# A decoder step with 32 streamed experts: tiles in one pipeline instead of pairs, nine weight blocks, seven pairs' rows picked by TensorE

## The reference, cut to what matters

```
x1 = LN1(alpha * x + Mixer(x))            # in-projection, pooling and short convolution, out-projection
g  = top-1 of 4 expert groups (x1 @ w_group + b_group), gate = softmax
e  = top-2 of the 8 experts of that group (x1 @ w_expert + b_expert), gates renormalised
f  = sum over the two experts e of gate * ((silu(x1 @ w1[e]) * (x1 @ w3[e])) @ w2[e])
y  = LN2(alpha * x1 + f)                  # eps 1e-5
w1, w3: 32 x (1024, 512) float32;  w2: 32 x (512, 1024) float32
```

## Time and profile before

| | us |
|---|---|
| median of three timed executions | 716.93 |
| the profiled execution: its time | 716.73 |
| its span on the core | 715.0 |
| PE busy in the span | 609.8 (85%) |
| DVE / ACT / POOL busy | 306.9 / 181.8 / 158.4 |
| DMA: moved, mean rate | 235.99 MB, 330 GB/s |
| of this the queue of indirect DMAs (q0) | 11.71 MB, 4.9% of 16 engines' span |
| mean granted TensorE clock | 0.961 |

### The profile page before, as it was taken

The page is one execution under the profiler, slowest core; times in us unless marked ns, Lnnn a source line. Parts: engine busy times, 40 slices in busy tenths (PEclk is TensorE's granted clock), DMA queues, the critical chain, the costliest instruction groups (busy, mean ns, idle before and its releaser), DMA issues.

```text
span 715.0 us, 10596 instructions
## 1 busy us (share of the span) xinstructions
PE 609.8 (85%) x4220; PEld 420.6 (59%) x4220; DVE 306.9 (43%) x787; ACT 181.8 (25%) x287; POOL 158.4 (22%) x181
## 2 busy tenths in 40 slices
PE   5999999999999999889877987988788777877771
PEld 5999999878775556446444544554344435453440
DVE  4462485517577133353442353342434251433244
ACT  3323313302111313223232323322232121223130
POOL 1000000000000414244235224332341322233142
PEclk9999999999989999999999999899999999999996
DMA  9952133834496999999999999999999999999950
GB/s 250 282 184 90 45 118 105 339 135 190 152 392 250 390 418 420 417 416 417 422 416 421 413 422 416 422 416 421 422 418 421 415 422 420 425 415 418 404 223 21
DMA packets 45738, 235.99 MB, mean 330 GB/s; under 512 B 13667, under 2 KB 18275, under 8 KB 28712
## 3 DMA queue, kind: packets, MB, share of 16 engines
q1 hardware_dynamic: 32287, 220.92, 76.6%
q0 software_dynamic: 12544, 11.71, 4.9%
q10 hardware_dynamic: 857, 2.67, 0.9%
HBM read 237.69 MB, written 30.20 MB: 375 GB/s over the span
## 4 chain that ended last, share of the span: by engine, by line
PE 34%; issue 19%; DMA 17%; SPq 15%; POOL 9%; DVE 5%; ACT 1%; POOLq 0%; DVEq 0%; ACTq 0%
PE ps L534 14%; SPq L402 9%; PE ps L591 7%; DMA tenth_block<-in_w 6%; DMA blocks<-in_w 6%; PE ps L694 6%; SPq L406 5%; PE ps L715 2%; POOL out L1085 2%; POOL out L1081 2%; POOL prev L1077 2%; POOL first_outputs L1073 2%; DMA first_outputs<-ye,first_row 2%; DMA x_tok<-in_x_prompt 1%; DMA prev<-first_outputs,final_row 1%
## 5 line engine op out<-in xcount | busy, mean ns | idle before, releaser
L694 PE MATMUL ps<-blocks,ln 128*64 128x256 f32 x1952 | 233.5, 396 | 53.6 <-DMA blocks<-in_w 32.4
L694 PEld LDWEIGHTS ps<-blocks,ln 128*64 128x64 f32 x1952 | 157.0, 143 | 130.2 <-issue 57.2
L715 PE MATMUL ps<-blocks,hT 128*64 128x512 f32 x464 | 105.7, 596 | 6.0 <-DMA blocks<-in_w 5.8
L1077 POOL DMA_INDIRECT prev<-first_outputs,final_row x32 | 34.9, 1091 | 246.7 <-DMA first_outputs<-ye_more,first_row 119.3
L715 PEld LDWEIGHTS ps<-blocks,hT 128*64 128x64 f32 x464 | 32.8, 137 | 59.8 <-issue 48.5
L798 ACT ACTIVATE ln<-ps 128x512 f32<-128x512 f32 (+1 forms) x38 | 19.9, 572 | 112.2 <-PE ps L682 89.0
L1494 DVE SCALAR_TENSOR_TENSOR h_rows<-silu,slot_gate,ps 128x256 f32<-128x256 f32 x33 | 15.7, 477 | 69.0 <-PE ps L694 68.9
L1499 DVE COPY hT<-ps 128x256 f32<-128x256 f32 x33 | 13.9, 422 | 71.1 <-PE ps L703 71.1
L534 PE MATMUL ps<-xT_high,w_in_high 128*128 128x288 f32 x256 | 41.4, 305 | 0.9 <-DVE xT_low L1187 0.9
L981 ACT ACTIVATE std<-rstd,eps 128x1 f32<-128x1 f32 x32 | 9.4, 295 | 125.3 <-DVEq L1523 125.2
L534 PE MATMUL ps<-xT_low,w_in_high 128*128 128x288 f32 x256 | 39.5, 297 | 0.0
(11 more groups left out here) (232 smaller groups left out, 789.6 us busy)
## 6 DMA issues: line engine op xcount, KB each, us to landing
blocks<-in_w SPq DMA_DIRECT2D x87, 2048.0 KB, 36.5
tenth_block<-in_w SPq DMA_DIRECT2D x9, 2048.0 KB, 37.9
blocks<-in_w_in SPq DMA_DIRECT2D x3, 2048.0 KB, 10.5
blocks<-in_w_out SPq DMA_DIRECT2D x2, 2048.0 KB, 7.8
x_tok<-in_x_prompt SPq DMA_DIRECT2D x4, 512.0 KB, 5.2
blocks<-in_w_in SPq DMA_DIRECT2D x4, 512.0 KB, 11.3
first_outputs<-in_x_prompt SPq DMA_DIRECT2D x4, 512.0 KB, 8.7
x_rows<-x_tok ACTq DMA_DIRECT2D x4, 512.0 KB, 2.7
```

Source lines behind the costliest of these rows:

```text
L694: mm = pe.matmul(ps[64 * g:64 * g + 64, bank, 0:FH], x, w[:, k, g * FH:(g + 1) * FH], start=(k == 0), stop=(k == KD - 1))
L715: mm = pe.matmul(ps[64 * g:64 * g + 64, BY, :], hT[:, k % 2, k // 2 * SLOTS:(k // 2 + 1) * SLOTS], w[:, k, g * DH:(g + 1) * DH], start=(k ...
L1077: return g.indirect_dma_start(out=prev[w], out_offset=None, in_=first_rows[:, :], in_offset=rows_at(idx), bounds_check=last_row, oob_is_er ...
```

## The change

The parts, in the order of the kernel:

1. **Early matmuls.** `project(c)` waits for the high part of its weights, and for the low part only ahead of the third product; the fourth token tile is turned after the first half of `project(0)`. `keep_warm` is spread: 4, 2, 15 and 2 products in place of 21 and 12.
2. **Router.** `mask` is made straight from the choices, ahead of `picked`; `hot_first` comes from `mask` and the counts (two operations of 5 columns, one of 10, a comparison of 320 columns per tile) in place of two comparisons of 640 columns and their sums. The two columns blocks that `make_hot` needs are kept in `pick_at`.
3. **One pipeline.** Every tile t from 2 to 30 does w1 of t, hidden rows of t - 1, w3 of t, `down` of t - 1; tiles 30 to 32 end with their own `down`. Loads follow this order. No tenth block: `x_tok` is kept to the end. Load 11 (w1 of tile 4) then waits for tile 1's w1, 12 for its w3, 13 for `down` of tile 0.
4. **Picked pairs.** For pairs 3, 5, ..., 15 the fetch by DMA goes; DVE makes one-hot columns (`make_hot`), TensorE multiplies them with the five token tiles (10 matmuls of 128 x 512 in float32), ACT copies the rows to `xe_of[1]` (`keep_xe`).
5. **POOL's order**: load(t - 1), store(t - 1), fetch (only pairs 1, 2, 4, 6, ..., 16), send(t - 2). ACT copies tile 1's rows ahead of its wait for the table, and `make order` comes first after `products(0)` on DVE. Of the memory cleared before the first fetch only `xe_odd` (1024 columns) stands ahead of it.
6. **End.** w2 of tile 32 comes as two DMAs, and `down` waits for the second halfway. DVE adds `ye` to `prev` ahead of the last product and then the product itself, and normalises at once (`last_final`).

```diff
+STAGGERED = E - 2
 def order_of_loads():
-    loads = [(kind, t) for t in range(2) for kind in ("w1", "w3", "w2")]
-    for m in range(1, PAIRS):
-        tiles = [t for t in (2 * m, 2 * m + 1) if t != SHARED + 1]
-        loads += [(kind, t) for t in tiles for kind in ("w1", "w3")] + [("w2", t) for t in tiles]
+    for t in range(E + 1):
+        loads += [(kind, t) for kind in ("w1", "w3")]
+        loads += [("w2", s) for s in ([t - 1] if t < STAGGERED else [t - 1, t] if t == STAGGERED else [t]) if s >= 0]
+HOME = [n % EARLY_BLOCKS for n in range(len(LOADS))]
+PICKED = list(range(3, PAIRS, 2))
...
+            for n in range(EARLY_BLOCKS, EARLY_BLOCKS + 2):
+                block_free(n)
+                load(n)
+            sp.wait_ge(order_ready, 1)
+            for n in range(EARLY_BLOCKS + 2, EARLY_BLOCKS + 4):
                 block_free(n)
                 load(n)
             sp.wait_ge(table_ready, 1)
...
-                pe.wait_ge(w_low, c + 1)
+                pe.wait_ge(w_high, c + 1)
...
+                        if a:
+                            pe.wait_ge(w_low, c + 1)
...
+            def pick_pair(m):
+                n = PICKED.index(m)
+                pe.wait_ge(hot_ready, n + 3)
+                pe.wait_ge(xe_kept, 2 * n + 2)
+                pe.wait_ge(y_filled, 2)
+                for g in range(2):
+                    for j in range(NT):
+                        mm = pe.matmul(ps[:, BX[g], :], hot[:, j, :], x_tok[:, j, g * DH:(g + 1) * DH],
+                                       start=(j == 0), stop=(j == NT - 1))
+                    mm.then_inc(fetched, 1)
...
+            def tile(t):
+                if t % 2 == 0:
+                    pe.wait_ge(xeT_ready, t + 2)
+                into_hidden("w1", *place("w1", t), t, t % 2)
+                if t <= STAGGERED:
+                    turn_hidden(t - 1)
+                into_hidden("w3", *place("w3", t), t, t % 2)
+                if t % 2:
+                    turn_pair((t + 1) // 2)
+                if t <= STAGGERED:
+                    down(*place("w2", t - 1), t - 1)
+                if t % 2 == 0 and (t + 2) // 2 in PICKED:
+                    pick_pair((t + 2) // 2)
...
+            for t in range(2, E):
+                if t % 2 and (t + 1) // 2 in PICKED:
+                    keep_xe((t + 1) // 2)
+                if t == E - 1:
+                    spread(t - 2)
+                silu_of(t)
+                if t % 2:
+                    keep_xeT((t + 1) // 2)
+                    fill((t + 1) // 2, 0)
+                if 2 < t < E - 1:
+                    spread(t - 2)
+                if t % 2 and t < E - 1:
+                    fill((t + 1) // 2, 1)
...
             for t in range(2, E):
-                store(t)
-                send(t - 1)
-                load(t + 1)
-                if t % 2 == 0 and t // 2 + 2 <= PAIRS:
+                load(t - 1)
+                store(t - 1)
+                if t % 2 == 0 and t // 2 + 2 <= PAIRS and t // 2 + 2 not in PICKED:
                     fetch(t // 2 + 2)
+                if t > 2:
+                    send(t - 2)
...
+            def last_final():
+                u, w = E % YR, (E - 1) % ZR
+                dve.wait_ge(prev_loaded[w], 16 * ((E - 1) // ZR + 1))
+                dve.wait_ge(y_filled, E + 1)
+                settled(v.tensor_tensor(prev[w], prev[w], ye[u], ALU.add))
+                dve.wait_ge(y_done, E + 1)
+                settled(v.tensor_tensor(prev[w], prev[w], ps[:, BY, :], ALU.add))
+                norm2(E, w, settled)
...
+            for t in range(2, STAGGERED + 1):
+                keep_hT(t - 1)
+                products(t)
+                add_y((t - 1) % YR, t - 1)
+                if t > 2:
+                    final(t - 2)
+                if t % 2 and (t + 3) // 2 in PICKED:
+                    make_hot((t + 3) // 2)
```

More of the change, by code:

```diff
@@ L197, in block_at @@
         def block_at(b):
-            return tenth[:, :] if b == EARLY_BLOCKS else blocks[:, b, :]
+            return blocks[:, b, :]
         def in_block(b):
@@ L407, in load_out, with block_free, expert_of, load @@
                              src.rearrange("(g p c) d -> p g c d", g=2, c=KF // 2)).then_inc(block_loaded[b], 16)
+            def block_free(n):
+                kind, t = LOADS[n - EARLY_BLOCKS]
+                sp.wait_ge({"w1": h1_done, "w3": h_done, "w2": y_done}[kind], t + 2 if t == SHARED else t + 1)
+            chosen = {}
+            def expert_of(t):
+                p = t if t <= SHARED else t - 1
+                if p < EARLY:
+                    return p
+                if t not in chosen:
+                    chosen[t] = sp.value_load(order[0:1, p:p + 1], min_val=0, max_val=E - 1)
+                return chosen[t]
+            def load(n):
+                kind, t = LOADS[n]
+                if kind == "w2" and t == E:
+                    e = expert_of(t)
+                    src = w2[bass.DynSlice(e, 1)].rearrange("e f d -> (e f) d").rearrange("(g p c) d -> p g c d", g=2, c=KF // 2)
+                    for g, landed in ((0, block_loaded[HOME[n]]), (1, last_loaded)):
+                        sp.dma_start(out_block(HOME[n])[:, 2 * g:2 * g + 2, :], src[:, g, :, :]).then_inc(landed, 16)
+                elif kind == "w2":
+                    load_out(HOME[n], expert_of(t))
+                else:
+                    load_in(HOME[n], {"w1": w1, "w3": w3}[kind], expert_of(t))
             for j in range(NT):
@@ L419, in _ @@
             sp.wait_ge(in_done, 16)
-            load_in(1, w3, 0)
-            load_out(2, 0)
+            load(1)
+            load(2)
             sp.wait_ge(in_dve, 8)
@@ L501, in turn_x @@
                     mm.then_inc(x_turned, 1)
-            for j in range(4):
+            for j in range(3):
                 turn_x(j)
@@ L607, in turn_x1, with keep_warm @@
                         mm.then_inc(x1_turned, 1)
+            def keep_warm(products):
+                for _ in range(products):
+                    pe.matmul(ps[:, 2, 0:P], ident[:, :], ident[:, :], start=True, stop=True)
             def route(j):
@@ L630, in _ @@
                 turn_x1(j - 1)
-            for j in range(NT - 2, NT):
-                route(j)
-                if j + 1 < NT:
-                    turn_x1(j + 1)
-            def keep_warm(products):
-                for _ in range(products):
-                    pe.matmul(ps[:, 0, 0:P], ident[:, :], ident[:, :], start=True, stop=True)
-            keep_warm(21)
+            pe.wait_ge(out_kept, NT + 3)
+            keep_warm(4)
+            route(NT - 2)
+            turn_x1(NT - 1)
+            keep_warm(2)
+            route(NT - 1)
+            keep_warm(15)
             pe.wait_ge(mask_ready, 1)
@@ L645, in _ @@
                 for j in range(i + 1):
-                    mm = pe.matmul(ps[:, 5, i * E:(i + 1) * E], before[:, :] if j == i else ones[:, :], mask[:, j, :],
-                                   start=(j == 0), stop=(j == i))
+                    r = ROWS[j]
+                    mm = pe.matmul(ps[:, 5, i * E:(i + 1) * E], before[0:r, :] if j == i else ones[0:r, :],
+                                   mask[0:r, j, :], start=(j == 0), stop=(j == i))
             mm.then_inc(pos_done, 1)
             for j in range(NT):
-                mm = pe.matmul(ps[:, 6, 0:E], ones[:, :], mask[:, j, :], start=(j == 0), stop=(j == NT - 1))
+                mm = pe.matmul(ps[:, 6, 0:E], ones[0:ROWS[j], :], mask[0:ROWS[j], j, :], start=(j == 0), stop=(j == NT - 1))
             mm.then_inc(count_done, 1)
@@ L771, in token_table @@
                 mm.then_inc(table_done, 1)
-            keep_warm(12)
-            first_pair()
-            for m in range(1, PAIRS):
-                pair(m)
-            pe.wait_ge(xeT_ready, 2 * PAIRS + 2)
-            last_tile()
+            keep_warm(2)
+            first_tiles()
+            for t in range(2, E + 1):
+                tile(t)
+                if t >= STAGGERED:
+                    turn_hidden(t)
+                    down(*place("w2", t), t, last_half if t == E else None)
             pe.wait_ge(extra_ready, 1)
```

254 lines of the change are left out of this document (109 added, 145 removed).

## The result

| | before | after |
|---|---|---|
| median of 20 timed executions each | 717.12 (714.07 to 720.48) | 719.20 (718.01 to 724.57) |
| the profiled execution: time, span | 716.73, 715.0 | 718.01, 716.2 |
| PE / ACT busy in the span | 609.8 / 181.8 | 658.6 / 226.0 |
| mean granted TensorE clock | 0.961 | 0.979 |

The ratio of the times is 1.0037, with a 95% interval of 1.0024 to 1.0051: 1.7 to 3.7 us slower, within the 0.5% that the prediction called no change, but on the other side of the forecast of 715.8. All times are in us.

A forecast was written before the change was run, and what follows sets the result against it. The experts' part was taken to go at the pace of the DMA weight stream. The sum was 716.73 - 0.5 + 6.5 - 6.0 - 0.9 = 715.8 us, in effect no change, with a range of 709 to 723.

The forecast's parts named there:

- early matmuls, start of the stream: First in-projection to early loads: first product starts earlier, out-projection and the four loads behind it move along, -0.5 us.
- early gap: Weight stream before about 237 us: load 11 waits for tile 1's w1, DMA engines idle longer, +6.5 us (3.5 to 8.5).
- fetches: Indirect-DMA queue in the experts' part: seven fetches, 2.06 MB, no longer take DMA time, -6.0 us.
- picks on TensorE: Tiles 2 to 32: seven pairs' matmuls, 60 us in all, lie beside the stream and cost nothing; without cover up to 60.
- end: Behind tile 32's last weights: one of two sums leaves the path, -0.9 us (0 to -2.5); split of w2 gives nothing.
- Late next is the same chain of normalisation and two sends: Close of the end term: what follows the last sum was taken as unchanged.
- One pipeline and POOL's order: Experts' tiles: a silu's wait behind a norm goes, POOL's cycle fits under the stream, nothing on the path: 0.
- its recipe: Early gap's idle time from load issue times, first data 0.9 us later, 5.0 us a block: 8.9 before, 15.2 after.
- the lead of 37 us: TensorE's cover at tile 32's w3: done at 657 if nothing else waits, by the stream at 695; 1.2 us a tile.
- rival with TensorE as the bound: Tiles 2 to 31: picks raise PE's work to 13.6 us a tile, 1.8 of idle stays: 732 us; chance 0.14.
- rival with 711.2: Weight stream: indirect DMAs cost the last engine more than their bytes (7.6 us), gap only +3.5: 711.2 us; chance 0.30.
- gap in full, fetches only bandwidth: Weight stream: gap costs +8.5, fetches bring -4.9, no gain at either end: 720.3 us; chance 0.10.

The follow-up runs named there:

- nine blocks: Kernel before without the tenth block, load 11 waiting for w1 of the last tile of the pair before: 721.69 us, ratio 1.0088 to the kernel before.
- two undo experiments: Kernel before without fetches of pairs 3, 5, ..., 15: 710.33 us, ratio 0.9894; changed kernel with two reorderings near its end, all fetches by DMA again: 722.88, 1.0074.
- no picks: Changed kernel with tile 31's norm behind tile 32's products, tile 30's copy moved earlier, and all pairs fetched by DMA: 722.88 us, ratio 1.0074 to the kernel before.
- both tail edits: Changed kernel with tile 31's norm behind tile 32's products and tile 30's hidden-row copy ahead of tile 28's norm: 716.12 us, ratio 1.0007 to the kernel before.
- the copy moved alone: Changed kernel with only tile 30's hidden-row copy put ahead of tile 28's norm on DVE: 718.55 us, ratio 1.0035 to the kernel before.

## Why the prediction was wrong

Step by step, as they stood in the sum:

| step | forecast | measured | from |
|---|---|---|---|
| early matmuls, start of the stream | -0.5 (0 to -2) | -2.75 in the profile, some 1.4 of it the clock; from -3.0 to +0.9 between profiles of this kernel and its variants | early loads at 186.00 to 189.92, before 189.00 |
| early gap | +6.5 (3.5 to 8.5) | +6.6 idle; an added 5.4 cost 5.3 to 6.3 | windows after; nine blocks |
| fetches | -6.0 (-4.9 to -7.6) | -7.6 by ratios (-6.0 to -9.3), -6.9 by medians, -5.5 in the profile; -4.8 to -8.0 in the new kernel | two undo experiments |
| picks on TensorE | 0 | none seen, 62.0 us of work | no picks |
| end | -0.9 (0 to -2.5) | +3.25 in the profile | end of w3 to end of span |

**The step that failed is the end**, with the sentence "Late next is the same chain of normalisation and two sends" and, ahead of it, the zero for "One pipeline and POOL's order". I followed the hidden rows through the new stream and asked only whether `final(t - 2)` finds its data in time. I did not write down the order of DVE and ACT for the last two tiles: two norms of about 4.6 us each stand ahead of the products of tile 32, and the silu of tile 32 behind the second square root. The kernel before had the products of its last tile ahead of such work. This was to be read in the diff without a chip. The gain named there did come: from the end of the last `down` to the end of the last norm it is 4.6 us, before 6.1. But the way from w3 to the end of `down` went from 5.5 to 11.0 us, 3.15 for the wait and 2.2 for the clock. So the term was +3.25 where -0.9 stood, and with one norm put behind the products it was -0.85. That kernel's time is 715.89, beside a forecast of 715.8; that the rest of the sum fits so closely is partly luck, since the price of the fetches is known only to 5 to 9 us, and the start, forecast at -0.5, differs by up to 3.9 between profiles.

**What was right.** The gap, by its recipe: load 11 was forecast for 236.5 and left at 235.17, the idle time was 6.6 us more where 6.5 stood. The picks: a pair costs 8.85 us of TensorE (8.6 forecast), and the lead of 37 us that was to be left is 22.3 us of waits, so TensorE came nearer to being the bound than I said; from 276 to 460 us it has no idle time at all, while the stream runs at 1.01. The rival with TensorE as the bound (732) is out. The rival with 711.2 may be right on the price of the fetches (7.6 by ratios, 5.5 in the profile) and was wrong on the gap (3.5, measured 6.6). The rival "gap in full, fetches only bandwidth" came nearest to the time (720.3), but not by its own sum: its gap of 8.5 is 1.9 more than was measured, its 4.9 for the fetches lies under the interval, and it knows nothing of the tail.

**What was undersized.** The start, in the profile. In the first 25 us TensorE stands idle between groups, and in some executions its clock is at the lower level for some of them. The same 16 matmuls in two profiles of the same changed kernel:

```profile
12.73 1.22 PE L534 MATMUL ps<-xT_low,w_in_high 128*128 128x288 f32 x8
13.78 1.22 PE L534 MATMUL ps<-xT_high,w_in_low 128*128 128x288 f32 x8
```

```profile
13.31 2.04 PE L534 MATMUL ps<-xT_low,w_in_high 128*128 128x288 f32 x8
15.15 1.98 PE L534 MATMUL ps<-xT_high,w_in_low 128*128 128x288 f32 x8
```

The early loads left at 186.25 in the first and at 189.92 in the second, and the spans are 716.2 and 719.8: 3.7 us at the start, 3.6 at the end. The kernel before was not at full clock there either:

```profile
14.15 2.27 PE L534 MATMUL ps<-xT_high,w_in_high 128*128 128x288 f32 x8
```

Its first 24 matmuls of this kind take 5.1 us, those of the first profile after 3.75. So some 1.4 of the 2.75 us are not the change's doing, and what is left lies within the bounds of 0 to 2.

With -2.75 + 6.6 - 7.6 + 3.25 on 716.73 the sum would have been 716.2, against 718.01 in the profile. With the 5.5 us that the profiles give for the fetches it is 718.3. So the account of the profiled execution closes within 0.3 us; that of the medians does not close better than the price of the fetches is known.

## What to carry to other kernels

When a change reorders the small engines' work to suit the steady state, write out the last two tiles' operations in the order of each queue, and ask of each one ahead of the last matmul whether it must be there: the same stall cost nothing 50 us before the end (the stream covered it) and 4 us behind the last landing. A bandwidth-bound stream pays most of every idle us, however early it lies (5.3 to 6.3 us for 5.4, 4.2 to 6.0 for 6.7), and of two ways to save bytes one may spend TensorE freely as long as PE still waits for weights. A stall just ahead of a critical group of matmuls is to be counted twice, once for its length and once for the clock that it costs.

## What the runs showed of the hardware

**The clock behind a short wait.** Sixteen matmuls of 128 x 512 take 3.65 us at the full level. Behind 3.81 us of idle PE, then two short matmuls and 0.61 us, they took 5.88 us; behind 5.37 us, 5.56 us. With the wait taken away they took 3.65 us. How much is lost varies: behind the same wait of 5.4 us the matmuls took 5.39 to 6.25 us in five profiles. A shorter wait can do it too, and need not: behind 2.24 us of waiting for weights the 32 matmuls of a w3 took 5.36 us in the kernel with both tail edits (granted 0.50 from 675 to 676); behind 2.37 us they took 3.67 with the copy moved alone. The Trainium skill, "TensorE: Matmul & The Clock Gate", section "HAM oscillation — how this bites in real kernels", tells of the same thing between tiles of a matmul kernel, a wait for DMA that makes the next tile start at the lower clock; the trace agrees, and here the waits were for DVE and for ACT.

**A start that varies.** Between executions of the same kernel the first matmuls ran at either level, worth up to 3.7 us at the other end of the kernel. A single profile of each of two kernels does not tell 0.5% apart unless such an offset is read first, here at SP's early loads.

**One core's stream is steady.** It moved 417 to 420 GB/s from 276 to 640 us with and without the fetches, picks and tenth block. At that rate the 2.21 MB of the seven fetches are 5.3 us; the profiles of the kernel before with and without them differ by 5.5, the timed runs by 6.9 to 7.6 (6.0 to 9.3). Whether a MB of gathered rows costs more than the 2.4 us of a MB of weights (171 us for 71.83 MB, rows 4) stays open.
